# Strassen's seven products for the FFN up projection, and a down projection in four rounds of its own

## The reference, cut to what matters

```python
def conv_ffn(h, w_up, conv_w, conv_b, w_down):
    u = h @ w_up                                   # 1024 -> 5632
    s = u.shape[1]
    up = jnp.pad(u, ((0, 0), (1, 1), (0, 0)))
    u = up[:, :s] * conv_w[0] + up[:, 1:s + 1] * conv_w[1] + up[:, 2:s + 2] * conv_w[2] + conv_b
    g, val = jnp.split(u, 2, axis=-1)
    return (jax.nn.silu(g) * val) @ w_down         # 2816 -> 1024

x = x + g_a * o
f = conv_ffn(modulate(x, norm_ffn[l], sh_f, sc_f), w_up[l], conv_w[l], conv_b[l], w_down[l])
x = x + g_f * f
```

## Time and profile before

| | |
|---|---|
| median of 3 runs | 3458.79 us |
| profiled execution, span of the core | 3458.0 us |
| matmuls | 20797, busy 3286.6 us (95%) |
| weight loads (PEld) | busy 3039.5 us (88%) |
| DVE, ACT, POOL busy | 55%, 34%, 28% |
| DMA | 229.8 MB, mean 66 GB/s |

### The profile page before, as it was taken

One profiled execution on the slowest core, in us unless ns is written; L12 is line 12 of the kernel. 1 busy time (PEld: TensorE's weight loads), 2 busy tenths in 40 slices (PEclk: granted clock), 3 DMA queues, 4 the chain that ended last, 5 costly groups with the idle time before them and its releaser, 6 DMA issues. The chain is left out here.

```text
span 3458.0 us, 51915 instructions
## 1 busy us (share of the span) xinstructions
PE 3286.6 (95%) x20797; PEld 3039.5 (88%) x20797; DVE 1885.8 (55%) x2760; ACT 1187.1 (34%) x2113; POOL 953.1 (28%) x730
## 2 busy tenths in 40 slices
PE   6899999997999999999998999998999999999997
PEld 4788888886999999999988887876799999999997
DVE  5565556664265455545555566666336555455455
ACT  4344444444241211222123566655423112221122
POOL 1122222222342222333233122222142223332221
PEclk9999999998999999999999999999999999999998
DMA  6333333423211111111113111101331111111101
GB/s 239 107 105 99 109 113 110 120 83 116 92 62 43 37 42 36 42 36 55 43 38 81 38 32 34 32 24 38 143 82 43 43 37 42 36 55 42 36 31 61
DMA packets 206661, 229.80 MB, mean 66 GB/s; under 512 B 30564, under 2 KB 173533, under 8 KB 205341
## 3 DMA queue, kind: packets, MB, share of 16 engines
q1 hardware_dynamic: 186973, 162.69, 15.6%
q10 hardware_dynamic: 11664, 42.47, 3.7%
q0 software_dynamic: 7856, 22.29, 1.8%
HBM read 181.79 MB, written 31.98 MB: 62 GB/s over the span
## 5 line engine op out<-in xcount | busy, mean ns | idle before, releaser
L192 PE MATMUL psum<-Hh,wh 128*128 128x384 f32 x3264 | 1110.6, 340 | 26.4 <-PEq L746 7.4
L194 PE MATMUL psum<-Hl,wh 128*128 128x384 f32 x3264 | 1097.1, 336 | 0.0
L193 PE MATMUL psum<-Hh,wl 128*128 128x384 f32 x3264 | 1096.7, 336 | 0.0
L311 DVE SCALAR_TENSOR_TENSOR x<-psum,mod,x 128x384 f32<-128x384 f32 (+2 forms) x768 | 376.8, 514 | 635.6 <-PE psum L194 599.9
L192 PEld LDWEIGHTS psum<-Hh,wh 128*128 128x128 f32 x3264 | 617.0, 189 | 39.7 <-issue 29.0
L193 PEld LDWEIGHTS psum<-Hh,wl 128*128 128x128 f32 x3264 | 617.2, 189 | 0.0
L194 PEld LDWEIGHTS psum<-Hl,wh 128*128 128x128 f32 x3264 | 616.3, 189 | 0.0
L910 POOL TENSOR_TENSOR wl<-wr,wh 128x1024 fp32r<-128x1024 f32 x88 | 219.9, 2498 | 973.6 <-ACT wh L806 973.6
L859 ACT ACTIVATE ff_u<-psum 128x768 f32<-128x768 f32 x86 | 70.0, 814 | 1084.6 <-PE psum L194 1084.6
L1077 DVE SCALAR_TENSOR_TENSOR ff_c<-ff_u,par,ff_c 128x1153 f32<-128x1153 f32 x172 | 371.7, 2161 | 15.6 <-DVE ff_c L1074 5.2
L192 PE MATMUL psum<-ff_ah,ff_dh 128*128 128x384 f32 x1056 | 365.1, 346 | 13.0 <-DVE x L311 8.2
(11 more groups left out here) (242 smaller groups left out, 4424.0 us busy)
## 6 DMA issues: line engine op xcount, KB each, us to landing
wr<-w_up SPq DMA_DIRECT2D x88, 512.0 KB, 3.8
ff_dr<-w_down SPq DMA_DIRECT2D x22, 1024.0 KB, 5.9
da_mw<-mod_w ACTq DMA_DIRECT2D x40, 512.0 KB, 3.8
wr<-mod_w ACTq DMA_DIRECT2D x40, 512.0 KB, 4.8
wr<-w_qkv_diff SPq DMA_DIRECT2D x24, 512.0 KB, 18.1
x<-x_save SPq DMA_DIRECT2D x16, 576.0 KB, 6.6
in_mw<-mod_w SPq DMA_DIRECT2D x8, 1024.0 KB, 10.9
Hh<-oh_save SPq DMA_DIRECT2D x14, 576.0 KB, 10.1
```

The lines of the kernel that those rows point to most:

```text
L192: pe.matmul(out, w_hi, m_hi, start=start, stop=False)
L193: pe.matmul(out, w_lo, m_hi, start=False, stop=False)
L194: return pe.matmul(out, w_hi, m_lo, start=False, stop=stop)
L311: last = dve.scalar_tensor_tensor(g.x[:, m, lo:hi], g.PS[:, bank, lo - n * NB:hi - n * NB], g.mod[:, gate + m, cond:cond + 1], g.x[:, m, l ...
```

## The change

In each layer:

- Pairs 0 and 1 are computed as before (`CLASSIC` = 2). For pairs 2 to 21 the product of a [gate; value] by channels matrix (cut 2 by 2: gate and value, channel chunks 0 to 3 and 4 to 7) with token blocks 0 and 1 is done by Strassen's method in Winograd's form: seven products P1 to P7 of 12 matmuls each. Token block 2 stays direct (`G` and `V`, 24 matmuls each). A pair has 7 x 12 + 2 x 24 = 132 matmuls.
- The token sums T1 to T4 (each 4 chunks of 128x384) are made once in a layer: T1, T2, T4 on DVE, T3 on POOL, their high parts on ACT, low parts on POOL (T4's on DVE). T2 to T4 are kept in `tf`, which has the memory of the residual `x`; so `x` is written to DRAM at the start and read back during the first down round.
- For each pair four sums of weight blocks (S1 to S4, 128x512 each) are made from the raw weights: on POOL for pair 2, on DVE from pair 3 on. The high and low parts are made of A1, A2 (the raw gate and value weights) and S12, S34: four splits of 128x1024 for a pair instead of two.
- Partial results are put together by ACT copies to `ev` (p1, p5, u2) that TensorE waits for before it adds to the same bank, and by three DVE additions of a bank and such a copy (`join`).
- The activation of every pair is written to DRAM (`act_save`). After the last pair the down projection runs in 4 rounds of 6 banks and 22 channel chunks: 88 units of 6 products (18 matmuls); the sum over all 22 chunks stays in PSUM, and DVE adds 24 banks per layer in place of 264. For each unit SP loads 128x768 of `w_down` and 128x384 (rounds 0 and 3) or 128x768 (rounds 1 and 2) of the activation, ACT and POOL split the weights, ACT and DVE the activation. Norm steps of `nx` are put among the last rounds.
- All loops are unrolled.

```diff
+                with nc.sbuf_tensor(f"tf_{layer}", [P, 3, 2, 4, NB], F32R) as tf:
+                    g.tf = tf
                 g.x = s.enter_context(nc.sbuf_tensor(f"x_{layer}", [P, KC, T], F32))
...
+CLASSIC = 2
+STRASSEN = ("P1", "P2", "P5", "P6", "G", "P7", "P3", "V", "P4")
+FORMS = {"P1": ("A11", "B11"), "P2": ("A12", "B21"), "P3": ("S4", "B22"), "P4": ("A22", "T4"), "P5": ("S1", "T1"),
+         "P6": ("S2", "T2"), "P7": ("S3", "T3")}
+CHAIN = {"P1": "X", "P6": "X", "P7": "X", "P4": "X", "P2": "Y", "P5": "Z", "P3": "Z"}
...
+        eng.tensor_tensor(s1, a21, a22, ALU.add).then_inc(b.summed, 1)
+        eng.tensor_tensor(s3, a11, a21, ALU.subtract).then_inc(b.summed, 1)
+        eng.wait_ge(b.summed, done + 1)
+        eng.tensor_tensor(s2, s1, a11, ALU.subtract).then_inc(b.summed, 1)
+        eng.wait_ge(b.summed, done + 3)
+        eng.tensor_tensor(s4, a12, s2, ALU.subtract).then_inc(b.summed, 1)
...
 # SP
+            for n in range(NN):
+                sp.wait_ge(b.added, 16 + 4 * n)
+                cols = slice(n * NB, (n + 1) * NB)
+                sp.dma_start(g.x_save[:, :, cols], g.x[:, :, cols]).then_inc(b.saved, 16)
+            next_gate(1)
+            next_value(1)
+            next_gate(2)
+            for p in range(1, LAST):
+                next_value(p + 1)
+                store(p - 1)
+                next_gate(p + 2)
...
 # ACT
+            classic_out(0, 0)
+            form_hi(1, "A1")
+            act.wait_ge(b.saved, 16 * NN)
+            act.wait_ge(b.xr_d, KC * NN)
+            t_high("T3", (0, 1))
+            classic_out(0, 1)
+            form_hi(1, "A2")
+            t_high("T1", range(4))
+            t_high("T3", (2, 3))
+            t_high("T2", range(4))
+            silu(0)
+            classic_out(1, 0)
+            for name in ("A1", "S12", "S34"):
+                form_hi(2, name)
+            classic_out(1, 1)
+            t_high("T4", range(4))
+            for p in range(CLASSIC, FC):
+                if p > CLASSIC:
+                    corner_out(p - 1)
+                piece_out(p, "p1")
+                form_hi(p, "A2")
+                piece_out(p, "p5")
+                piece_out(p, "u2")
+                silu(p - 1)
+                if p < LAST:
+                    form_hi(p + 1, "S12")
+                    third_out(p, 0)
+                    form_hi(p + 1, "A1")
+                    form_hi(p + 1, "S34")
...
 # POOL
+            pool.wait_ge(b.hi_d, 2 * KC)
+            pool.wait_ge(b.lo_d, 2 * KC)
+            for step in range(3):
+                for k in range(4):
+                    t_sum(pool, b.t_pool, "T3", k, step)
+            t_low("T3", (0, 1))
+            form_lo(1, "A1")
+            form_lo(1, "A2")
+            t_low("T1", range(4))
+            t_low("T3", (2, 3))
+            t_low("T2", range(4))
+            pool.wait_ge(b.t_lo, T_LOW_AT["T3", 3])
+            form_sums(pool, CLASSIC)
+            for name in ("A1", "S12", "S34"):
+                form_lo(2, name)
+            for p in range(CLASSIC, FC):
+                form_lo(p, "A2")
+                if p < LAST:
+                    for name in ("S12", "A1", "S34"):
+                        form_lo(p + 1, name)
+            for q in range(UNITS_DN):
+                down_lo(q)
...
 # PE
+            def quarter(step, bank):
+                (wh, wl), (mh, ml) = weight_form(FORMS[step][0]), token_form(FORMS[step][1])
+                out, fresh = PS[:, bank, 0:NB], step in OPENS
+                for k in range(4):
+                    pe.matmul(out, wh[:, k, :], mh[:, k, :], start=fresh and k == 0, stop=False, skip_group_check=not fresh)
+                    pe.matmul(out, wl[:, k, :], mh[:, k, :], start=False, stop=False, skip_group_check=not fresh)
+                    last = pe.matmul(out, wh[:, k, :], ml[:, k, :], start=False, stop=k == 3, skip_group_check=not fresh)
+                last.then_inc(b.mm, 1)
...
+            first_ups()
+            for p in range(1, CLASSIC):
+                classic(p)
+            for p in range(CLASSIC, FC):
+                strassen(p)
+            for q in range(UNITS_DN):
+                down(q)
...
 # DVE
+            for name, steps in (("T1", 3), ("T2", 2)):
+                for step in range(steps):
+                    for k in range(4):
+                        if name == "T2" and step == 0:
+                            dve.wait_ge(b.t_vec, 8 + k + 1)
+                        t_sum(dve, b.t_vec, name, k, step)
+            convs(0, 0)
+            convs(0, 1)
+            mult(0)
+            # ... T4 in two steps, its low parts once ACT has made the high ones
+            convs(1, 0)
+            convs(1, 1)
+            mult(1)
+            for p in range(CLASSIC, FC):
+                if p > CLASSIC:
+                    convs(p - 1, 1)
+                    mult(p - 1)
+                if p < LAST:
+                    form_sums(dve, p + 1)
+                for name in ADDS:
+                    join(p, name)
+                if p < LAST:
+                    convs(p, 0)
```

More of the change, by code:

```diff
@@ new lines, in piece_out, with third_out @@
+            def piece_out(p, name):
+                step, i, last = {"p1": ("P1", 0, "C11"), "p5": ("P5", 1, "C22"), "u2": ("P6", 2, "C12")}[name]
+                act.wait_ge(b.mm, MM_AT[p, step])
+                if p > CLASSIC:
+                    act.wait_ge(b.joined, ADD_AT[p - 1, last])
+                act.activation(b.ev[:, i, :], PS[:, pair_banks(p)[CHAIN[step]], 0:NB], ACT.Copy).then_inc(b.copied, 1)
+            def third_out(p, v):
+                act.wait_ge(b.mm, MM_AT[p, "GV"[v]])
+                u_free(p, v)
+                tail_out(p, v, 3 * v)
@@ new lines, in _ @@
+            corner_out(LAST)
+            silu(LAST)
+            for q in range(3, UNITS_DN):
+                down_hi(q)
+                act_hi(q)
+                if not nx:
+                    continue
+                if q == FC + 4:
+                    act.wait_ge(b.prod, FC)
+                    act.wait_ge(stored[LAST % 2], 32 * (FC // 2))
+                e = ROUND * ((q - 4) // FC - 1) + (q - 4) % FC
+                if q - 4 >= FC and (q - 4) % FC < ROUND:
+                    act.wait_ge(b.dn_add, e + 1)
+                    nx.square(act, e)
+                if 71 <= q < 79:
+                    if q == 71:
+                        act.wait_ge(b.dn_mm, ROUND * (ROUNDS_DN - 1))
+                    nx.high(act, 0, q - 71)
+                if q >= 83:
+                    nx.high(act, 1, q - 83)
@@ L897, in _ @@
+                    unit_done(act, UNITS_DN - 6 + j)
+                    act.activation(g.wh[:, j, :, :], g.wr[:, j, :, :], ACT.Copy).then_inc(b.w_hi, 1)
+                for k in range(UNITS_DN - 83, KC):
+                    nx.high(act, 1, k)
+                for e in range(ROUND * (ROUNDS_DN - 1), KC * NN):
+                    act.wait_ge(b.dn_add, e + 1)
+                    nx.square(act, e)
+                for k in range(KC):
+                    nx.high(act, 2, k)
         @block.gpsimd
@@ new lines, in _ @@
+            form_sums(pool, CLASSIC)
[8 more added lines that the diff above has]
+                down_lo(q)
+                if not nx:
+                    continue
+                e = ROUND * ((q - 4) // FC - 1) + (q - 4) % FC
+                if q - 4 >= FC and (q - 4) % FC < ROUND:
+                    nx.add(pool, e)
+                if q == 57:
+                    nx.root(pool, 0)
+                if q == 79:
+                    nx.root(pool, 1)
@@ new lines, in convs, with mult, join @@
+            def convs(p, v):
+                for step in range(3):
+                    conv(p, v, step)
+            def mult(p):
+                dve.wait_ge(b.conv, 3 * (2 * p + 1) + 3)
+                dve.wait_ge(b.silu, p + 1)
+                dve.tensor_tensor(c_slot(p, 1), c_slot(p, 0), c_slot(p, 1), ALU.mult).then_inc(b.prod, 1)
+            def join(p, name):
+                step, part, i, v, at = {"C11": ("P2", "p1", 0, 0, 0), "C22": ("P7", "p5", 1, 1, NB), "C12": ("P3", "u2", 2, 0, NB)}[name]
+                dve.wait_ge(b.mm, MM_AT[p, step])
+                dve.wait_ge(b.copied, COPY_AT[p, part])
+                dve.wait_ge(b.conv, 3 * (2 * (p - 1) + v) + 3)
+                dve.tensor_tensor(b.u[:, v, 1 + at:1 + at + NB], PS[:, pair_banks(p)[CHAIN[step]], 0:NB], b.ev[:, i, :],
+                                  ALU.add).then_inc(b.joined, 1)
@@ L1178, in _ @@
+            act_lo(1)
+            conv(LAST, 0, 2)
+            conv(LAST, 1, 0)
+            act_lo(2)
+            conv(LAST, 1, 1)
+            conv(LAST, 1, 2)
+            mult(LAST)
+            for q in range(UNITS_DN):
+                if q + 3 < UNITS_DN:
+                    act_lo(q + 3)
+                if q % FC == FC - 1 and q < UNITS_DN - 1:
+                    for e in range(ROUND * down_round(q), ROUND * (down_round(q) + 1)):
+                        add_down(e)
                 if not nx:
```

754 lines of the change are left out of this document (464 added, 290 removed).

## The result

The changed kernel takes 3402.68 us (median of four runs, 3400.51 to 3404.59) against 3458.28 (3452.32 to 3459.57): a ratio of 0.984, with a 95% interval of 0.9826 to 0.9854, so 1.6% less. The forecast was 3409. The profiled execution has a span of 3402.8 us, 55.2 less than before's.

The account below looks back on a forecast made before the run. TensorE, busy 95% of the span, was taken as the bound. Span: 3458.0 - 84.3 + 4 + 50 + 3 - 21.4 + 3 - 4 = 3408.3 us, so a median of 3409; range 3370 to 3462.

Parts of the forecast that it names:

- The matmuls: FFN pairs: 12 fewer matmuls a pair, 480 in all at 0.1756 us each, 84.3 us saved.
- the 0.1 us added for a pair: Steady Strassen pairs: an allowance for an occasional late addition, 4 us in all.
- The matmul rate: Whole phase: matmuls might run at 0.1733 us in place of 0.1756, between 0 and -20 us; -4 taken.
- The start of a layer: Norm block 1 to pair 3: TensorE idles while DVE and POOL share work, 25 us a layer, 50 in all.
- the walk of turns: Layer start, DVE and POOL step by step: P1 of pair 3 at 1069, against 1066 by their 90 us of work.
- Entry, changes of round, last units: Down rounds: entry and three round changes 1 us a layer, last four units 1 us; in all 3 us.
- DMA in the rounds: Down rounds 1 and 2: 249 GB/s at a DMA share of 0.78 fits, cost 0; +18 a layer as other end.
- Rival 2: Down rounds: DMA sets the pace, at 220 GB/s +36 us for two layers, 3445 us; chance 0.11.
- The ends: Last group's down matmuls of each layer: waits on the last activation go, 17.3 + 4.1 = 21.4 us saved.
- the norm's tail: Layer 0, last down matmul to next phase: 31.5 us in place of 28, 3 us more.
- Rival 1: Steady pairs: DVE and POOL's shared port pair sets the pace, 26.7 us a pair, 3542 us; chance 0.15.
- rival 3: Layer start: DVE and POOL use each other's gaps better, cost 12 us a layer, 3383 us; chance 0.14.

Follow-up runs that it names:

- edges: Changed kernel with DVE's down-projection order altered: unit 3's activation low split before the last pair's last tap, round-end additions before unit q+3's split; 3386.34 us.
- pad12: Changed kernel with P1's 12 matmuls issued twice in every Strassen pair, so 144 matmuls a pair; 3478.88 us.
- less12: Changed kernel with the V product of token block 2 over 4 of its 8 chunks only, so 120 matmuls a pair; 3328.19 us.

## Why the prediction was right, and where its terms were off

The time, 3402.7, is 6.3 us under the forecast. The mechanism held: TensorE sets the pair, the start of a layer leaks, the ends come back. The sizes held less well: the start and the matmul rate came out 32 us cheaper than forecast, the rounds 21 us dearer. That the sum is within 6 us of the span is luck.

- **The matmuls**, -84.3: the count is 480. The steady pair is 23.00 us against 132 x 0.1736 = 22.92, so the 0.1 us added for a pair was right.
- **The matmul rate**, -4: mis-sized. It is 0.1736 us each (576 in 100 us) in place of 0.1756, and over some 4,370 matmuls a layer that is -17.5 for both layers, near the end that I had put at -20. Where it was lost before is in the groups of PE's weight loads from 1110 to 1480, the kernel before and then the changed one:

```profile
L192 PEld LDWEIGHTS psum<-ff_ah,ff_dh 128*128 128x128 f32 x240 | 45.0, 187 | 5.6 <-DVE x L311 3.4
```

```profile
L195 PEld LDWEIGHTS psum<-Hh,wh 128*128 128x128 f32 x256 | 48.1, 188 | 0.0
```

  In 25 of the 120 down banks of that stretch the first weight load waited for DVE's addition out of the bank, five times 0.67 us and twenty times 0.11, 5.6 us in 370 (the row names only the five long ones, 3.4). PE's own row shows 1.8 of that, so I had taken the rest for noise. The change has no down banks among the pairs. With 370/0.1736 - 370/0.1756 = 24 matmuls or 4 us, the size is near; no run isolates it, so the cause of the better rate is not shown.
- **The start of a layer**, +25 each: 16.4 measured in layer 0 (P1 of pair 3 at 1058.3, and this run was 1.4 us earlier at norm block 1, so 14.7 later than the 1045 of TensorE alone, with 1.7 of half speed behind it), 14.7 in layer 1. The step that failed is the walk of turns. A1 of pair 1 came at 1006.1, about where it was forecast (1005), though through another turn: DVE's twenty sums let POOL in only at 1000.3. Norm block 2 was 4 us late, not 7. The waits named behind it, for A1, P6 and P4 of pair 2, didn't come: TensorE had no lead left to lose. The sum of 90 us from norm block 1 to P1 of pair 3 was 83.4, nearer than the walk's 93.
- **Entry, changes of round, last units**, +3: mis-sized by 21. Over 1,530 matmuls from unit 3 on (265.6 us at 0.1736) layer 0 took 280.4 and layer 1 275.3, so 14.8 and 9.7. In layer 0, 24 short matmuls of the next norm, some 2.7 us, are among them. I had looked at what the engines have to do in a unit, and not at what stands ahead of it in DVE's queue; `edges` took back some 16 of it.
- **DMA in the rounds**, 0: right, and with far more room than the row allowed. Rival 2 is out. The Trainium skill, SBUF — State Buffer, section "A bandwidth-pool intuition that's wrong", gives 358 GB/s from HBM to a core, as half of a stack's 716. Here one core ran alone; the 392 of the run with extra loads is above that, and the measurement decides.
- **The ends**, -21.4, and the norm's tail, +3: 30.7 us from the last down matmul's successor (1788.16) to the next phase (1818.89) against 27.9 before, and no wait of 5 us before it. Right, though the parts that the prediction names for its 31.5 (12.6, a fourth bank of 4.2, and 11.4) add up to 28.2.
- **Rival 1** is out by `pad12` and `less12`, **rival 3**, 12 a layer, was nearly the case for the start alone. From norm block 1 to the next phase the terms of layer 0 add up to -42.1 - 8.7 + 16.4 + 1.5 + 14.8 - 17.3 + 2.8 = -32.6 (matmuls, rate, start, pairs, rounds, end, tail), and the trace has -30.9. For layer 1, from norm block 1 to the last down matmul, they give -29.0 (with 14.7, 9.7 and -4.1 for start, rounds and end) against -28.0. These 2 and 1 us I can't place. The rest of the 55.2 lies outside these stretches: 1.4 less ahead of layer 0's norm block 1, 3.4 more between the layers (750.2 against 746.8 us, in attention, whose cause is open) and 1.7 more at the end.
- **Readings of the rows.** The share of 70% before, beside which the prediction set its 91%, is too high: from 1110 to 1410 the SBUF work of DVE and all of POOL's add up to 178 of 300 us, 59%, and at least one of the two is at such work in 140, 47%; in the changed kernel it is 259, 86%. And the low part "under 0.6 us" is 0.62 in the earlier trace rows. Neither moves the sum.

DVE's taps, as foreseen, pay for the sharing; by line, in ns, min/median/max, beside the earlier trace rows:

```profile
L1507 DVE SCALAR_TENSOR_TENSOR ff_c<-ff_u,par,ff_c x176: 1401/1904/3647, 1001.8 to 3094.5; 128x1153 f32<-128x1153 f32 x176
L1247 POOL TENSOR_TENSOR wl<-wr,wh x88: 2390/2509/3492, 953.2 to 3070.6; 128x1024 fp32r<-128x1024 f32 x88
```

## What to carry to other kernels

When engines exclude each other, bound a start-up phase by the work that they share in the stretch where both have some, and don't add up the waits met on a walk: taking away the largest wait (8.9 us) gave nothing, since it was where a lead ran out, while taking away shared work gave 5.7 us of that stretch, of which 3.6 reached the next stage. Move such work to the engine that holds the shared resource for the shorter time, or into a stretch where its partner works on PSUM. In an in-order queue look at what stands ahead of the item that the next stage needs: two reorderings of VectorE's queue brought 16 us.
